# Expert value products: the weight rests of a tile multiplied one tile later

## What is computed

```
act = gelu(x . u_e)                 # for the picked experts e
y   = sum over e of gate_e * act_e * v_e
```

## Time and profile before

| what | value |
|---|---|
| median of 3 runs (lowest to highest) | 1797.89 us (1795.83 to 1799.44) |
| the profiled execution | 1800.65 us |
| its span in the profile | 1798.9 us |
| TensorE busy with matmuls | 1746.3 us, 97% |
| VectorE, ScalarE, GpSimd busy | 1252.2, 941.9, 490.8 us |
| share of TensorE in the chain of work that ended last | 83% |
| matmuls of the values stage | 1536 (three kinds, 512 each), 1050.2 to 1405 us |

### The profile page before, as it was taken

How to read it: one execution, slowest core, us unless ns; L and a number is a source line. 1 busy time by engine, 2 the same in 40 slices (tenths; PEclk the granted TensorE clock), 3 DMA queues, 4 the chain that set the end, 5 groups by cost and what they waited for, 6 DMA issues and landing times.

```text
span 1798.9 us, 33010 instructions
## 1 busy us (share of the span) xinstructions
PE 1746.3 (97%) x11190; PEld 1549.7 (86%) x11190; DVE 1252.2 (70%) x2360; ACT 941.9 (52%) x1389; POOL 490.8 (27%) x224
## 2 busy tenths in 40 slices
PE   9999989999999999999999999999999999999997
PEld 6799878897878999999999988888888677669996
DVE  4667577776424499157777578888888896667777
ACT  5476576534555544567777643333333575334444
POOL 4256733501568588810000000000000000003332
PEclk9999989999999999999999999999999999999999
DMA  6654443577344477756555687767777783355553
GB/s 216 218 180 141 166 139 110 192 243 268 125 164 152 132 221 230 226 176 175 173 175 173 194 265 238 234 235 238 238 236 234 273 273 109 118 179 183 185 186 117
DMA packets 122839, 347.63 MB, mean 193 GB/s; under 512 B 13904, under 2 KB 46800, under 8 KB 122512
## 3 DMA queue, kind: packets, MB, share of 16 engines
q1 hardware_dynamic: 121248, 339.52, 58.0%
q0 software_dynamic: 1520, 7.21, 1.1%
HBM read 328.84 MB, written 17.83 MB: 193 GB/s over the span
## 4 chain that ended last, share of the span: by engine, by line
PE 83%; DVE 6%; ACT 4%; POOL 2%; issue 2%; DMA 2%; DVEq 0%; SPq 0%; ACTq 0%; POOLq 0%
PE banks L934 82%; POOL weight_rest L852 2%; ACT arena L1681 2%; DMA weight_ring<-in_stream 1%; ACT weight_high L1681 1%; PE banks L945 1%; DVE weight_rest L2313 1%; DVE ssd_rest L2339 1%; ACT span_exponentials L1681 0%; ACT L1681 0%; DVE attention_rest L2599 0%; DVE arena L2997 0%; ACT scratch L1681 0%; DMA residual<-in_x 0%; DVE arena L2351 0%
## 5 line engine op out<-in xcount | busy, mean ns | idle before, releaser
L1681 ACT ACTIVATE weight_high<-weight_ring 128x1024 fp32r<-128x1024 f32 x448 | 472.9, 1057 | 451.8 <-PE banks L934 343.3
L852 POOL TENSOR_TENSOR weight_rest<-weight_ring,weight_high 128x1024 fp32r<-128x1024 f32 x165 | 414.3, 2520 | 266.5 <-ACT weight_high L1681 152.5
L2313 DVE TENSOR_TENSOR weight_rest<-weight_ring,weight_high 128x1024 fp32r<-128x1024 f32 x283 | 346.0, 1224 | 157.3 <-ACT weight_high L1681 154.3
L934 PE MATMUL banks<-a_high,weight_high 128*128 128x256 f32 x1216 | 304.0, 288 | 0.2 <-ACT weight_high L1681 0.2
L934 PE MATMUL banks<-a_rest,weight_high 128*128 128x256 f32 x1216 | 297.8, 283 | 0.0
L934 PEld LDWEIGHTS banks<-a_high,weight_high 128*128 128x128 f32 x1216 | 232.6, 191 | 1.5 <-issue 1.1
L934 PEld LDWEIGHTS banks<-a_rest,weight_high 128*128 128x128 f32 x1216 | 232.9, 192 | 0.3 <-issue 0.2
L934 PE MATMUL banks<-weight_high,gated_high 128*128 128x512 f32 x512 | 201.2, 393 | 0.0
L934 PE MATMUL banks<-weight_high,gated_rest 128*128 128x512 f32 x512 | 200.2, 391 | 0.0
L934 PE MATMUL banks<-a_high,weight_rest 128*128 128x256 f32 x1216 | 170.9, 283 | 2.4 <-POOL weight_rest L852 2.4
L934 PE MATMUL banks<-x_high,weight_high 128*128 128x256 f32 x672 | 167.1, 286 | 4.7 <-DVE x_rest L3085 3.7
(11 more groups left out here) (361 smaller groups left out, 3105.6 us busy)
## 6 DMA issues: line engine op xcount, KB each, us to landing
weight_ring<-in_stream SPq DMA_DIRECT2D x512, 512.0 KB, 3.5
arena<-in_stream SPq DMA_DIRECT2D x66, 512.0 KB, 3.3
unit_spill<-small SPq DMA_DIRECT2D x128, 128.0 KB, 3.6
scratch<-unit_spill SPq DMA_DIRECT2D x128, 128.0 KB, 3.2
residual<-in_x SPq DMA_DIRECT2D x2, 512.0 KB, 4.1
arena<-in_mem POOLq DMA_DIRECT2D x2, 512.0 KB, 5.3
arena<-in_ctx POOLq DMA_DIRECT2D x2, 512.0 KB, 5.0
arena<-in_keys POOLq DMA_DIRECT2D x1, 1024.0 KB, 5.2
```

What stands on the lines that cost most here:

```text
L852: nc.gpsimd.tensor_tensor(w_lo[:, e % 2, :], raw(e)[0], w_hi[:, e % 2, :], ALU.subtract).then_inc(S["rest_ready"], 1)
L934: return nc.tensor.matmul(out, lhsT, rhs, start=start, stop=stop, skip_group_check=True)
L1681: return nc.scalar.activation(out, in_, f, **kw)
L2313: tt(w_lo[:, e % 2, :], raw(e)[0], w_hi[:, e % 2, :], ALU.subtract).then_inc(S[ready], 1)
```

## The change

The rest products of tile `a - 1` are done together with the high products of tile `a`: for each of the four banks, first the rest product of the tile before, then the two high products of this tile. So a bank gets three products in a row, and the order of banks in a tile is 0 0 0 1 1 1 2 2 2 3 3 3. Tile 0 has eight products only, tile 125 is followed by its own four rest products, and the last two tiles keep their order.

The signals move with it. `hi_begun` rises in tile `a` with the last rest product of tile `a - 1`, which is the tenth product of twelve (and once in tile 0, once behind tile 125). `hi_used` rises with the twelfth product instead of the eighth. At the head of a tile TensorE now waits for three things: the gated activations of this tile, its high weights, and the rest weights of the tile before.

```diff
+            def rest_products(a, t, h):
+                return mm(bank(("y", t, h)), gated_hi[:, a % 4, tsl(t)], w_lo[:, (V0 + a) % 2, h * 512:(h + 1) * 512],
+                          start=False, stop=False)
+
+            def values(a, turn=None):
 
                 i_ = 0 if turn is None else turn
                 e = V0 + a
                 pe.wait_ge(S["p_ready"], i_ * 4 + (a + 1))
-                ready, count = rest_count(e)
-                split_sums(e, "y", gated_hi[:, a % 4, :], gated_lo[:, a % 4, :], turn, 4, ready, i_ * 4 + count, last)
-
+                pe.wait_ge(S["hi_ready"], i_ * 4 + (e + 1))
+                if a:
+                    ready, count = rest_count(e - 1)
+                    pe.wait_ge(ready, i_ * 4 + count)
+                for t in range(TT):
+                    for h in range(2):
+                        o, w = bank(("y", t, h)), w_hi[:, e % 2, h * 512:(h + 1) * 512]
+                        if a:
+                            ins = rest_products(a - 1, t, h)
+                            if t == h == 1:
+                                ins.then_inc(S["hi_begun"], 1)
+                        ins = mm(o, gated_hi[:, a % 4, tsl(t)], w, start=False, stop=False)
+                        if a == t == h == 0:
+                            ins.then_inc(S["hi_begun"], 1)
+                        ins = mm(o, gated_lo[:, a % 4, tsl(t)], w, start=False, stop=False)
+                ins.then_inc(S["hi_used"], 1)
+
+            values(0)
             with pe.Fori(0, P // 4 - 1) as i:
-                for a in range(4):
+                for a in range(1, 5):
                     values(a, i)
-            for a in range(P - 4, P - 2):
-                values(a)
+            values(P - 3)
+            pe.wait_ge(*rest_count(V0 + P - 3))
+            for t in range(TT):
+                for h in range(2):
+                    ins = rest_products(P - 3, t, h)
+            ins.then_inc(S["hi_begun"], 1)
...
-                        if h == 0 and t == a - (P - 2):
+                        if h == 0 and t == 1 and a == P - 1:
                             ins.then_inc(S["hi_begun"], 1)
```

More of the change, by code:

```diff
@@ L1409, in _, with split_sums @@
                     units(U_EARLY + U_GATED + j, ("u3", j), i)
-            def split_sums(e, name, hi, lo_, turn, n, rest_ready, rest_count, last=False):
+            def split_sums(e, name, hi, lo_, turn, n, rest_ready, rest_count):
                 def high(w):
@@ L1426, in rest @@
                             ins = mm(bank((name, t, h)), hi[:, tsl(t)], w[:, h * 512:(h + 1) * 512],
-                                     start=False, stop=last)
-                            if last:
-                                filled(ins, (name, t, h))
+                                     start=False, stop=False)
                 split_tile(e, turn, n, high, rest, rest_ready, rest_count)
-            def values(a, turn=None, last=False):
+            def rest_products(a, t, h):
+                return mm(bank(("y", t, h)), gated_hi[:, a % 4, tsl(t)], w_lo[:, (V0 + a) % 2, h * 512:(h + 1) * 512],
+                          start=False, stop=False)
+            def values(a, turn=None):
                 i_ = 0 if turn is None else turn
```

## The result

The changed kernel takes **1804.05 us** (median of 11 runs, 1797.53 to 1806.19) against 1798.97 us (11 runs, 1793.7 to 1800.28) for the kernel before on the same chip: a ratio of 1.0023, 95% interval 1.0013 to 1.0032, so 2.3 to 5.8 us **slower**. The forecast was 1791.2 with a range up to 1798.2. The profiled execution took 1803.82 us.

A forecast was written before the change was run, and what follows sets the result against it. TensorE's product spacing was taken to bound the stage: 126 tiles x 0.054 = 6.7 us saved, other terms nothing. 1800.65 - 6.7 = 1793.9 like the profiled execution; medians lie 2.8 lower, so 1791.2, range 1789.8 to 1798.2.

The forecast's parts named there:

- Part (2): Waits at the head of a values-stage tile: later signals leave 0.5 us or more to spare, cost nothing.
- Part (3): The ring of weight fetches: released 2.1 us later against TensorE, still 4 us to spare, cost nothing.
- Part (4): Ends of the values stage: products moved, not added; the scaling chain behind moves along, so the gain is kept.
- part (1): Product spacing in the values stage: four bank changes instead of eight, tile 2.774 to 2.720 us, 126 tiles gain 6.7 us.
- The second witness: `spans` stage: bank changes after every pair, 230 ns a product, 3.3 over 226.7, taken as 6.7 ns a change.
- free rest products: `down` stage: a tile's four rest products take 0.91 us, as if bank changes cost nothing after long visits.
- (b): Values stage: banks don't matter, spacing belongs to operand alternation or place; tile stays 2.774 us, time 1797.9; chance 0.20.
- (d): Waits at the tile's head bite, needing more than 1.7 us of lateness; counted with (c), together 0.08.
- (c): Values stage: each turn between weight tiles costs 13.4 ns; tile 2.827 us, 6.7 us slower, 1804.6; chance 0.08 with (d).
- the 231 that were to decide: Sign for (c): distance behind a `weight_rest` product over 231 ns on average in the new order.
- (a): Values stage: plain price per bank change, eight become four, 27 ns a tile, 3.4 us gained, 1794.5; chance 0.28.

The follow-up runs named there:

- phases: Block left out; 35 sections of 96 products alone, addresses of loaded and moving operands varied against each other: 226.67 ns a product where equal, changed order at kernel's addresses 233.33.
- company: Block left out; 96 products at the kernel's addresses, its other work added one by one: 231.11 ns a product in the order of before and the changed order.
- addresses: Block left out; 18 sections of 96 products alone, mainly sweeping the address of `gated_high`: 226.67 ns a product at 128, changed order at the kernel's addresses 231.1.
- patterns: Block left out; sixteen orders of 96 products each alone on TensorE, `gated_high` at 128 past a multiple of 512: all 226.67 ns a product.
- sections 8 to 13: Products alone with all four operands at 0, at 64 or at 192, in both orders: 226.67 ns a product in all six.
- the two kernels with the pad: Kernel before and changed kernel, each with 192 spare bytes moving `gated_high` to 128 past a multiple of 512: 1792.87 and 1792.34 us, against 1799.25 for before.
- before_two_banks: Kernel before with both feature halves of a token half summed into one bank: 1796.21 us in one run, tile 2.773 us.
- after_two_banks: Changed kernel with one bank for each token half: 1803.9 us in one run, tile 2.800 us.

## Why the prediction was wrong

**What held.** TensorE alone bounds the stage, and only the spacing matters: the chain is still one piece of it. Part (2): no wait at the head of a tile, and VectorE's wait names TensorE, 0.45 us a time where 0.36 was worked out for a shorter tile. Part (3): no wait for the ring. Part (4): the end of the stage moves with its last product; TensorE then waits 0.64 us for VectorE's scaling, where it was 0.52:

```profile
1411.97 1.09 PE L945 MATMUL banks<-const,scratch 128*128 128x128 f32 x8 [0.64 <-DVE scratch L2872]
```

**What failed: part (1), the spacing.** The sum had a tile fall from 2.774 to 2.720 us, 6.7 us less in all; it rose to 2.800, 3.4 us more in the stage. "A change costs some 6.7 ns, and the third and each later product of a visit can take that up" was drawn from three stages. `split_block` and the values stage were said to differ in the order of the banks; they also differ in where the loaded operand lies: `x_high` on the phase of the weights, `gated_high` 64 bytes off it. The 6.7 ns were real, one step of the pattern, and eight of them in a tile; that there are eight bank changes in it is chance, since with two banks they stayed. The second witness, `spans`, is no witness for banks either: of the fifteen products of the earlier trace rows every second loads the second `log_gates_high`, at 320, which lies 64 bytes off the other way, and in `phases` one pair of operands with that difference had 228.9 ns. And `down`, whose free rest products I took for the tail of long visits, has all its operands on one phase. The forecast's figure of 2.720 us a tile was right as the floor of this stage; the lever for it was an address.

**The rivals.** (b), "to where they lie", had the cause of the extra with a chance of 0.20, but put the time at no change. It left out that where the phases differ a change can put the stretch into another pattern: 12 steps a tile instead of 8. The order of the products is not shown to be what did it. With the order of before and the moved waits and signals there were 11 steps, and the changed order alone had 8 in `company` and `addresses` and 12 in `phases`. So (d), which took waits to cost only where TensorE has to stand and wait, was short as well. (c), at 1804.6, comes within 1 us of the result by a mechanism that isn't there: `patterns` and sections 8 to 13 of `phases` turn between the weight tiles with every bank at 226.67 ns, and the changed kernel with equal phases turns between them at 2.720 us a tile. Even its sign came true: the distances behind a rest product are 235, 233, 235 and 233, 234 on average, over the 231 that were to decide. That it comes so near is luck; a number that hits doesn't show its mechanism. (a) fell with the two-bank kernels.

**What was in the rows.** The earlier trace rows gives 0.94 us for the four rest products, which the prediction took for 235 ns each; by whole nanoseconds they are 934, 233.5 each, and the eight products ahead of them 230.0 each. All four load `gated_high`, of the eight only every second does, and in `phases` that load beside a weight tile, over and over, has 233.3. So the operand could have been suspected before the bank.

**What stays open.** Why 256 bytes, and why a difference of 192 costs 2.2 ns a product and one of 96 7.6; what picks the pattern, and so why the moved waits and signals gave 11 steps a tile and the whole change 12, when no section outside the kernel shows such an effect of them. A version in which the changed order falls into the cheaper pattern in the kernel wasn't tried, since equal phases beat every pattern seen.

## What to carry to other kernels

Where matmuls of one shape have two spacings in two stages at the same granted clock, with no wait in either, compare the operands' addresses before the order: put the loaded and the moving operand on the same place within 256 bytes, by a pad. A change of order, waits or signals that is judged while the phases differ is judged by an accident: here it cost 27 ns a tile, and with equal phases nothing. And before one rule is fitted to three stages, list everything in which they differ, the addresses too.

## What the runs showed of the hardware

- A float32r matmul of 512 columns starts every 226.67 ns where the stationary and the moving operand have the same address within 256 bytes, and every 228.9 to 234.4 where they don't, for every difference tried in steps of 32 bytes; the extra comes in steps of 6.67 ns over a repeating pattern. At equal phases neither banks nor the order changed it (`patterns`, and the two kernels with the pad). At the kernel's addresses the number of banks changed nothing (`before_two_banks`, `after_two_banks`), and for the order of before neither did signals, waits, or the work of VectorE, ScalarE and the transfers (`company`). The Trainium skill, "SBUF — State Buffer", section "Operand start alignment", lets an operand start at any multiple of its element size and says that this is about legality, not speed; all the addresses here keep to that rule, and they differ by up to 7.8 ns a product.
- 226.67 ns are 213.3 (512 columns at 2.4 GHz) and 13.3. The Trainium skill, "TensorE: Matmul & The Clock Gate", section "Back-to-back issue gap", gives 2.5 instead of the 13.3 for what it calls an isolated matmul, and some 131 ns a matmul in a sustained stream; no section of any run here came below 226.67.
- The spacing repeats exactly: 125 tiles of the changed kernel took 2800 ns each. At unequal phases products and addresses don't fix it: the same list at the same addresses took 2773 ns a tile in the kernel before and 2793 with the waits and signals moved, and the same 96 products alone took 231.11 ns each in one kernel and 233.33 in another, on another chip.
